# Differential attention: output projection in half chunks between the heads, first scores beside the last value chunk, one pair of score banks

## The reference, cut to what matters

```python
q, k, v = jnp.split(h @ w_in, 3, axis=-1)
q = rope_partial(q.reshape(B, T, H, 2, dh), cos, sin) * (dh ** -0.5)
k = rope_partial(k.reshape(B, T, H, 2, dh), cos, sin)
...
    s = jnp.einsum('bhiqd,bhikd->bhiqk', qb, k[:, :, :, :L]).astype(f32)
    p = jax.nn.softmax(jnp.where(mask, s, -jnp.inf), axis=-1)
    a = p[:, :, 0] - lam * p[:, :, 1]
    outs.append(jnp.einsum('bhqk,bhkv->bhqv', a.astype(v.dtype), v[:, :, :L]))
o = rmsnorm(jnp.concatenate(outs, axis=2), subln_g) * (1.0 - lambda_init)
return o.transpose(0, 2, 1, 3).reshape(B, T, D_MODEL) @ w_o
```

## Time and profile before

| | us |
|---|---|
| median of 3 runs | 1465.49 (1459.67 to 1471.15) |
| span of the profiled execution | 1462.9 |
| PE busy | 1402.7 (96%) |
| DVE busy | 937.9 (64%) |
| ACT busy | 664.8 (45%) |
| POOL busy | 81.7 (6%) |
| mean granted TensorE clock | 0.972 |

### The profile page before, as it was taken

How to read it: one execution, slowest core, us unless ns; L and a number is a source line. 1 busy time by engine, 2 the same in 40 slices (tenths; PEclk the granted TensorE clock), 3 DMA queues, 4 the chain that set the end, 5 groups by cost and what they waited for, 6 DMA issues and landing times.

```text
span 1462.9 us, 20830 instructions
## 1 busy us (share of the span) xinstructions
PE 1402.7 (96%) x8456; PEld 1229.0 (84%) x8456; DVE 937.9 (64%) x1128; ACT 664.8 (45%) x809; POOL 81.7 (6%) x150
## 2 busy tenths in 40 slices
PE   6999899999999999999899999999999999999996
PEld 2797799998787779999698878899998987899996
DVE  4797776785886667555585445676776423677774
ACT  2543444444445354444434354554545456545452
POOL 1021100100210100000100010000000000000000
PEclk9899999999997699999999999999999999999998
DMA  9696466864793147555355434454553530555440
GB/s 376 248 366 224 139 242 252 309 236 171 282 356 125 52 159 263 195 184 195 116 202 180 168 141 173 144 202 173 196 179 136 210 115 14 188 178 197 173 144 29
DMA packets 46092, 279.23 MB, mean 191 GB/s; under 512 B 5200, under 2 KB 5200, under 8 KB 18880
## 3 DMA queue, kind: packets, MB, share of 16 engines
q1 hardware_dynamic: 33264, 231.57, 44.2%
q0 software_dynamic: 12752, 46.57, 8.6%
HBM read 277.07 MB, written 1.05 MB: 190 GB/s over the span
## 4 chain that ended last, share of the span: by engine, by line
PE 90%; DVE 4%; ACT 2%; DMA 1%; issue 1%; POOL 1%; SPq 0%; POOLq 0%; DVEq 0%; ACTq 0%
PE ps L1566 41%; PE ps L1603 13%; PE ps L1604 12%; PE ps L1605 12%; DMA ada<-in_ada_w 1%; PE ps L1853 1%; DVE h_lo L986 1%; PE ps L1665 1%; PE ps L1627 1%; POOL rstd L499 1%; PE ps L1987 1%; PE ps L2001 1%; PE ps L1638 1%; DVE x L1027 1%; DVE h_hi L985 1%
## 5 line engine op out<-in xcount | busy, mean ns | idle before, releaser
L932 DVE TENSOR_TENSOR w_lo<-raw,w_hi 128x2048 fp32r<-128x2048 f32 x210 | 479.8, 2290 | 213.6 <-ACT w_hi L575 212.7
L575 ACT ACTIVATE w_hi<-raw 128x2048 fp32r<-128x2048 f32 x210 | 400.8, 1911 | 335.9 <-PE ps L1566 289.0
L1603 PE MATMUL ps<-h_hi,w_hi 128*128 128x256 f32 x1536 | 437.2, 285 | 6.0 <-DVE h_lo L986 5.3
L1604 PE MATMUL ps<-h_lo,w_hi 128*128 128x256 f32 x1536 | 435.4, 283 | 0.0
L1605 PE MATMUL ps<-h_hi,w_lo 128*128 128x256 f32 x1536 | 435.3, 283 | 0.0
L1603 PEld LDWEIGHTS ps<-h_hi,w_hi 128*128 128x128 f32 x1536 | 293.4, 191 | 11.4 <-issue 6.3
L1604 PEld LDWEIGHTS ps<-h_lo,w_hi 128*128 128x128 f32 x1536 | 293.5, 191 | 2.0
L1605 PEld LDWEIGHTS ps<-h_hi,w_lo 128*128 128x128 f32 x1536 | 293.6, 191 | 0.0
L1566 PE MATMUL ps<-w_hi,h_hi 128*128 128x512 f32 x448 | 151.6, 400 | 1.0 <-DVE h_lo L986 1.0
L1566 PE MATMUL ps<-w_lo,h_hi 128*128 128x512 f32 x448 | 148.2, 392 | 0.0
L1566 PE MATMUL ps<-w_hi,h_lo 128*128 128x512 f32 x448 | 147.6, 390 | 0.0
(11 more groups left out here) (249 smaller groups left out, 1173.3 us busy)
## 6 DMA issues: line engine op xcount, KB each, us to landing
raw<-in_stream SPq DMA_DIRECT2D x210, 1024.0 KB, 4.9
ada<-in_ada_w POOLq DMA_DIRECT2D x80, 512.0 KB, 6.5
ada<-in_ada_w SPq DMA_DIRECT2D x8, 512.0 KB, 12.5
raw<-in_ada_w SPq DMA_DIRECT2D x8, 512.0 KB, 16.1
row<-in_gate_b POOLq DMA_DIRECT2D x3, 512.0 KB, 3.7
x<-in_x SPq DMA_DIRECT2D x1, 1024.0 KB, 9.5
retc<-in_retc POOLq DMA_DIRECT2D x1, 1024.0 KB, 5.1
out<-xn SPq DMA_DIRECT2D x2, 512.0 KB, 2.7
```

The source lines that it names most:

```text
L575: act.activation(w_hi[:, s, :], raw[:, s, :], ACT.Copy).then_inc(hi_done[s], 1)
L932: dve.tensor_tensor(w_lo[:, s, :], raw[:, s, :], w_hi[:, s, :].bitcast(f32), ALU.subtract)\
L1603: pe.matmul(out, wh, h_hi[:, kt, :], start=kt == 0, stop=False)
L1604: pe.matmul(out, wh, h_lo[:, kt, :], start=False, stop=False)
```

## The change

The score banks are 6 and 7 for head 1 and 4 and 5 for all others, so that scores of head h wait for the exponentials of head h-1 (head 2: of head 0). Scores 0 and 1 stand ahead of the last value chunk and scores 2 behind it. Transposes and output of a head share bank 6, so the transposes of head h wait for `do_free`, the copy of the output of head h-1, which ACT now does ahead of the squares; the squares read the copy in SBUF. The result is transposed in pairs of heads through bank 7 (`d_pair` on PE, ACT and DVE). From head 3 on, PE does half an output chunk (12 matmuls, `do_half`) between the scores and the output of a head, and the sixth half behind the last pair. Conversions, low halves and ada steps move with it; POOL's loads of steps 88 and 89 move behind its roots. The number of matmuls, exponentials and bytes stays.

```diff
--- before.py
+++ after.py
@@ -220,6 +220,7 @@
         d_a = at("d_a", 2304, [2, 3 * P])
         d_at = at("d_at", 3072, [2, 3 * P])
         d_st = at("d_st", 3840, [3, 3, 4])
+        d_sq = nc.alloc_sbuf_tensor_at("d_sq", [P, 2, TT, P], f32, offset=nc.sbuf_base)
         d_o = at("d_o", 10240, [TT, D])
         lamv = at("lamv", 10240, [256])
         lamp = at("lamp", 10496, [2, 64])
@@ -336,6 +337,7 @@
         dat_done = sem("dat_done")
         do_mm = sem("do_mm")
         do_act = sem("do_act")
+        do_free = sem("do_free")
         drs = sem("drs")
 
         rs_mm = sem("rs_mm")
@@ -423,7 +425,7 @@
 
         def d_bank(h):
 
-            return (2, 4, 6)[h % 3]
+            return 6 if h == 1 else 4
 
         def s_bank(p):
 
@@ -532,13 +534,13 @@
             norm(2)
 
             gate_bias(1)
-            for s in range(8 * KT, 10 * KT + 6 + ADA_RING):
+            for s in range(8 * KT, 10 * KT + 4 + ADA_RING):
                 ada_load(s)
 
             for h in range(DH_):
                 pool.wait_ge(do_act, h + 1)
                 inverse_rms(stat[:, 1, 2 * h:2 * h + 2], stat[:, 0, 2 * h:2 * h + 2], 2, DDV).then_inc(drs, 1)
-            for s in range(10 * KT + 6 + ADA_RING, 11 * KT + ADA_RING):
+            for s in range(10 * KT + 4 + ADA_RING, 11 * KT + ADA_RING):
                 ada_load(s)
             norm(3)
             gate_bias(2)
@@ -751,12 +753,10 @@
             read_y(Y_DK, d_k)
             hi(C_DK + 7)
             d_features(d_qt, 0)
-            hi(C_DV + 4)
-            hi(C_DV + 5)
+            hi(C_DO)
             d_features(d_kt, 4)
-            hi(C_DV + 6)
             act.preload_act_table_set("natural_log_exp_and_others")
-            read_y(Y_DV, d_v)
+            hi(C_DO + 1)
 
             def d_exp(h):
 
@@ -772,23 +772,38 @@
             def d_out(h):
 
                 act.wait_ge(do_mm, h + 1)
-                out = ps[:, 0, (h % 2) * T:(h % 2 + 1) * T].rearrange("p (t k) -> p t k", t=TT)
+                out = ps[:, 6, 0:T].rearrange("p (t k) -> p t k", t=TT)
+                act.activation(d_o[:, :, h * DDV:(h + 1) * DDV], out, ACT.Copy).then_inc(do_free, 1)
+                act.wait_ge(do_free, h + 1)
                 for t in range(TT):
-                    act.activation(h_lo[:, 2 * (h % 2) + t, 0:DDV], out[:, t, :], ACT.Square,
-                                   accum_out=stat[:, 0, 2 * h + t:2 * h + t + 1])
-                act.activation(d_o[:, :, h * DDV:(h + 1) * DDV], out, ACT.Copy).then_inc(do_act, 1)
-
-            for h in range(3):
-                d_exp(h)
-            hi(C_DV + 7)
+                    last = act.activation(d_sq[:, h % 2, t, :], d_o[:, t, h * DDV:(h + 1) * DDV], ACT.Square,
+                                          accum_out=stat[:, 0, 2 * h + t:2 * h + t + 1])
+                last.then_inc(do_act, 1)
+
+            def d_pair(b):
+
+                act.wait_ge(tr_done, 4 * TR_DO + b + 1)
+                act.activation(h_hi[:, 2 * b:2 * b + 2, :].rearrange("p k t -> p (k t)"), ps[:, 7, :], ACT.Copy)\
+                    .then_inc(hh_done, 1)
+
+            d_exp(0)
+            d_exp(1)
+            hi(C_DO + 2)
+            read_y(Y_DV, d_v)
+            d_exp(2)
+            hi(C_DO + 3)
             for h in range(DH_):
+                if h % 2 and h > 1:
+                    d_pair(h // 2 - 1)
                 d_out(h)
                 if h + 3 < DH_:
                     act.wait_ge(da_done, h + 1)
                     d_exp(h + 3)
-            split_stage(TR_DO, h_hi)
-            for c in range(C_DO, C_DO + 3):
-                hi(c + 4)
+                if h == 5:
+                    hi(C_DO + 4)
+            hi(C_DO + 5)
+            d_pair(3)
+            hi(C_DO + 6)
             act.wait_ge(gsc_done, 4)
             norm(3, X_DIFF, TR_N3, C_DO + 7, lambda kt: gsc[:, 3 * KT + kt:3 * KT + kt + 1],
                  lambda kt: mod[:, (6 + SH_C) * KT + kt:(6 + SH_C) * KT + kt + 1])
@@ -1308,13 +1323,11 @@
                     steps(9 * KT + 2 * e, 2)
             dve.wait_ge(*(y_read(Y_DK, 3)))
             rotate(d_k, rope_k)
-            for e in range(4):
-                if e < 3:
-                    lo(C_DV + e + 4)
-                if e == 0:
-                    finish_part(9, 4)
-                if e < 2:
-                    steps(10 * KT + 3 * e, 3)
+            finish_part(9, 4)
+            lo(C_DO)
+            steps(10 * KT, 2)
+            lo(C_DO + 1)
+            steps(10 * KT + 2, 2)
 
             def d_maxima(h):
 
@@ -1348,7 +1361,7 @@
                 dve.wait_ge(dat_mm, h + 1)
                 if h >= 2:
                     dve.wait_ge(do_mm, h - 1)
-                dve.tensor_copy(d_at[:, h % 2, :], ps[:, 1, 0:3 * P]).then_inc(dat_done, 1)
+                dve.tensor_copy(d_at[:, h % 2, :], ps[:, 6, 0:3 * P]).then_inc(dat_done, 1)
 
             def d_scale(h):
 
@@ -1359,23 +1372,38 @@
                                                     ALU.mult, ALU.mult)
                 last.then_inc(o_done, 1)
 
+            def d_pair(b):
+
+                dve.wait_ge(hh_done, 4 * TR_DO + b + 1)
+                dve.tensor_tensor(h_lo[:, 2 * b:2 * b + 2, :].rearrange("p k t -> p (k t)"), ps[:, 7, :],
+                                  h_hi[:, 2 * b:2 * b + 2, :].rearrange("p k t -> p (k t)").bitcast(f32),
+                                  ALU.subtract).then_inc(hl_done, 1)
+
             d_maxima(0)
             d_maxima(1)
             d_combine(0)
+            d_combine(1)
+            lo(C_DO + 2)
             d_maxima(2)
             for h in range(DH_):
+                if h % 2 and h > 1:
+                    d_pair(h // 2 - 1)
                 d_transposed(h)
-                if h + 1 < DH_:
-                    d_combine(h + 1)
+                if h + 2 < DH_:
+                    d_combine(h + 2)
                 if h + 3 < DH_:
                     d_maxima(h + 3)
                 if h >= 1:
                     d_scale(h - 1)
+                if h == 4:
+                    lo(C_DO + 3)
+                if h == 5:
+                    steps(10 * KT + 4, 2)
+                if h == 6:
+                    steps(10 * KT + 6, 2)
             d_scale(DH_ - 1)
-            split_stage(TR_DO, h_lo, h_hi)
-            lo(C_DV + 7)
-            steps(10 * KT + 6, 2)
             lo(C_DO + 4)
+            d_pair(3)
             norm_scale(3, 6 + SC_C)
             lo(C_DO + 5)
             row_gate(1)
@@ -1842,12 +1870,11 @@
             pe.wait_ge(mod_done, 10)
             d_transposes(d_k, 4)
             h_rows(C_DV + 2, 2, 4)
-            h_rows(C_DV + 3, 3, 4)
 
             def d_scores(h):
 
-                if h >= 3:
-                    pe.wait_ge(ds_exp, h - 2)
+                if h >= 2:
+                    pe.wait_ge(ds_exp, 1 if h == 2 else h)
                 for i in range(2):
                     f, b = slice(i * DDH, (i + 1) * DDH), d_bank(h) + i
                     pe.matmul(ps[:, b, 0:T], d_qt[f, h, P:T], d_kt[f, h, :], start=True, stop=True)
@@ -1859,31 +1886,71 @@
 
             pe.wait_ge(mask_done, 1)
             pe.wait_ge(dtr_act, 8)
-            pe.wait_ge(*y_read(Y_DV, 3))
-            for h in range(3):
-                d_scores(h)
-            for h in range(DH_):
-                par = h % 2
+            d_scores(0)
+            d_scores(1)
+            h_rows(C_DV + 3, 3, 4)
+            d_scores(2)
+
+            def d_turn(h):
+
                 pe.wait_ge(da_done, h + 1)
                 if h:
-                    pe.wait_ge(dat_done, h)
+                    pe.wait_ge(do_free, h)
+                else:
+                    pe.wait_ge(ds_exp, 2)
                 for j in range(3):
-                    last = pe.transpose(ps[:, 1, j * P:(j + 1) * P], d_a[:, par, j * P:(j + 1) * P], ident)
+                    last = pe.transpose(ps[:, 6, j * P:(j + 1) * P], d_a[:, h % 2, j * P:(j + 1) * P], ident)
                 last.then_inc(dat_mm, 1)
+
+            def d_output(h):
+
+                pe.wait_ge(dat_done, h + 1)
+                if h == 0:
+                    pe.wait_ge(*y_read(Y_DV, 3))
+                v = lambda t: d_v[:, t, h * DDV:(h + 1) * DDV]
+                o = lambda t: ps[:, 6, t * P:(t + 1) * P]
+                a = lambda j: d_at[:, h % 2, j * P:(j + 1) * P]
+                pe.matmul(o(1), a(0), v(0), start=True, stop=False)
+                pe.matmul(o(1), a(1), v(1), start=False, stop=True)
+                pe.matmul(o(0), a(2), v(0), start=True, stop=True).then_inc(do_mm, 1)
+
+            def d_pair(b):
+
+                pe.wait_ge(o_done, GH_ + 2 * b + 2)
+                if b:
+                    pe.wait_ge(hl_done, 4 * TR_DO + b)
+                for j in range(2):
+                    for t in range(TT):
+                        kt = 2 * b + j
+                        last = pe.transpose(ps[:, 7, j * T + t * P:j * T + (t + 1) * P],
+                                            d_o[:, t, kt * P:(kt + 1) * P], ident)
```

(37 more changed lines are left out.)

## The result

The changed kernel takes 1478.6 us (median of 4, 1477.4 to 1480.0) against 1466.0 (median of 4); the ratio is 1.0097, 95% interval 1.0061 to 1.0133. By the medians that is 12.6 us slower, where 13 were forecast. (The ratio is not formed from the two medians, which would give 1.0086; the interval holds both.) The span of the profiled execution is 1475.6, 12.7 more.

The account below looks back on a forecast made before the run. PE at half its clock was taken to bound the heads. Waits in the new order gave +10.4 us, or +15.0 with more half clock; the middle, +13, on the median 1465.49 made 1478.5, range 1464 to 1489.

Parts of the forecast that it names:

- Links: In the heads, scores wait for the previous head's exponentials: 8.31 us a head at half clock, 6.07 at full.
- Start: Scores 0 to 2 and last value chunk: head 3's scores then wait 3.3 us for late exponentials, until 460.4.
- Halves: Half output chunks between scores and output lengthen the heads, filling no wait there; gate row at 528.2, 10.4 later.
- half (0,0): First half output chunk, behind head 6's scores: 12 matmuls, 5.1 us at half clock, bringing the full clock back at its end.
- Turn 4: Head 7's scores, a half chunk, head 4's output: until 504.0; wholly at half clock 4.6 us more.
- the middle that I took: Between full clock and half clock in the turn with head 7's scores, +10.4 and +15.0 us in all: +13.
- half (1,0): Half output chunk behind head 7's scores and head 4's output; waits for the second transposed pair of heads until 508.3.
- pair 3: Last transposed pair of heads: waits 2.8 us behind head 7's output for squares, POOL's roots and scaling.
- half (2,0): Half output chunk ahead of head 7's output: waits some 2 us for the third transposed pair, ends at 518.8.
- The clock at the end: Last turns to gate row: full clock, 2.72 us a half chunk; rival of half clock nearly throughout, about +21, chance 0.27.
- two cases of the clock: Half clock in heads 0 to 3 only, +10.4 us, or also with head 7's scores, +15.0; together chance 0.50.
- Moved for nothing: Moved ada steps, conversions and loads on DVE, POOL and SP add 0; uncovered, 2.7 us a turn or 2.3 at most.

Follow-up runs that it names:

- fillers: Changed kernel plus 34 matmuls whose result nobody reads, in PE's waits ahead of the scores of heads 3 to 7; ratio 1.0045 to the kernel before.
- both edits: Changed kernel with a second pair of score banks and the half chunk behind the head's output; 0.9969 of the kernel before, and 0.9969 when run again.
- the second pair alone: Changed kernel with heads 3 and 5 using score banks 2 and 3, no other engine's order changed; 1.0067 of the kernel before.

## Why the prediction was right

*Links.* Worked out at 8.31 us, measured 8.33 and 8.32; at the full clock 6.07 against 5.87 with fillers. Two pairs of banks took the waits ahead of the scores away, and that one pair makes them is shown. In time it is shown by both edits together, 0.9969 with an interval far below that of the changed kernel, and not by the second pair alone.

*Start.* PE waited 2.54 us ahead of scores 3, not 3.3, and scores 0 to scores 3 took 15.37, not 16.4. The timeline of ACT in the changed kernel has the reason, beside the earlier trace rows:

```profile
436.18 2.06 ACT L745 ACTIVATE d_kt<-ps 128x512 f32<-128x512 f32 x4 [6.51 <-PE ps L1852]
438.26 1.28 ACT L758 ACT_TABLE_LOAD   x1
439.55 1.92 ACT L577 ACTIVATE w_hi<-raw 128x2048 fp32r<-128x2048 f32 x1
```

ACT read d_k from 436.18 and no more from 438.88, so C_DO+1 was converted by 441.5 where I had 444.1. The change leaves one conversion ahead of the features where two stood, and I walked the queue with both. Of these 2.6 us, 1.3 are the lead that PE had there, which I didn't forecast: the kernel before stood at a clock of 0.50 from 430 to 433, the changed one at 1.00:

```profile
425.00:444.00 19.00, 18.45 (x98) 15.16 (x96) 12.60 (x25) 7.17 (x7) 2.12 (x4) 1.00 0.74 282
```

That lead is chance as far as the profiles tell: two of one kernel, the one with both edits, have scores 0 at 446.63 and at 443.46. The maxima of head 2 were then released by their scores (455.38) and not by DVE's chunk.

*Halves.* Scores 6 to scores 7: 12.9 forecast, 11.87 measured, since the clock came back inside half (0,0), at 489.8, and not at its end. Turn 4 fell once more, from 496.5 to 500, within its half: 7.24 to the end of its output, where 5.8 was the full clock, 10.4 the half one and 8.1 the middle that I took. The waits ahead of half (1,0) and pair 3 were 2.93 and 2.90 against 3.3 and 2.8; the one ahead of half (2,0) was 1.32 where I had named 2.

*The clock at the end.* I gave it no fall behind turn 4. There were two: half (1,0) took 4.45 and half (2,1) 5.26 where I had 2.72, 4.3 more together. So the sum holds by terms that cancel: 1.2 earlier ahead of the stage, start -1.0, three links -0.6 (24.3 against 24.9), scores 6 to 7 -1.0, scores 7 to the gate row +3.6 (36.2 against 30.0 and the 2.6 of the middle). That leaves -0.2: the gate row is at +12.8 (530.62 against 517.79), +13 forecast. The waits carry the result, in the links and ahead of halves and pairs, and both kinds were walked. That it is this close is luck: the lead of 1.2 us, the early start and the late falls of the clock were all missed and cancel, and +13 itself was the middle of two cases of the clock.

*Moved for nothing.* The ada steps in turns 5 and 6 do hold up DVE's copy once the half chunk stands behind the output; in the changed kernel they lie hidden, as said. *The clock rule.* The Trainium skill's TensorE: Matmul & The Clock Gate, HAM oscillation, ties the throttle to idleness of the array. The traces agree only in part. The three late falls of the changed kernel each came behind rests of PE, 2.3 to 4.1 us in all. But 0.50 stood over 24 us with no idle time in the kernel before, and 0.99 with a quarter of the time idle on 128 rows. The Trainium skill's rule on rotating banks (Perfetto Trace Analysis, Optimizing Tensor Performance) is borne out by the waits of the run with a second pair.

*What stays open.* How the clock's fall is timed: executions of one kernel put it at different heads (the kernel with both edits was profiled at 1460.7 and at 1452.6). What held the clock at 0.50 in the old heads. And what each single edit is worth in time.

## What to carry to other kernels

Before work is threaded between dependent steps, write down one round of the ring (here scores, output, copy, exponentials) and see whether the new work lies on it or beside it: moving the same half chunk off it gave 4 to 7 us. A buffer given up for the new work must be counted in that ring, and banks that are idle until the new work starts can serve until then. Where the clock is at half with PE fully busy, look at which matmuls fill it, and not only at gaps. Where the clock moves from execution to execution, compare the waits of two orders as well as their times.

## What had not been expected

- Heads with score matmuls on 64 rows ran at a granted clock of 0.50 without a gap. With the same columns on 128 rows they ran at 0.99, and the scores of a head took 1.55 us at the full clock instead of 2.34. That it is the rows is not shown: with fillers the scores on 64 rows ran at 1.00.
- 34 matmuls that nobody reads made the changed kernel 5 to 8 us faster.
- One kernel's executions differ by 15 us (1462.3 to 1477.4 with two pairs of banks) and by 20 (1450.2 to 1470.4, the kernel before on the same chip), and in the profiles the clock falls at different heads.
